# Around both down projections of a two-layer decoder step: one weight split and one gate eviction change their place

## Chip, core, metric

The kernel runs on one core of one Trainium2 chip. The metric is the time of one execution in microseconds (us), lower is better. All engines of the core (PE, which is TensorE; DVE; ACT; POOL; and SP, which here only issues DMAs) run their own instruction lists and meet at semaphores.

## What is computed

Two layers (L = 0 and 1) over 576 tokens (512 of a prompt, 8 x 8 of samples) of width 1024, in float32. Each layer is `x += mixer(rmsnorm(x)); x += convglu(rmsnorm(x))`; the mixer of layer 0 is an mLSTM, that of layer 1 attention with a window. The part of interest is the second half of each layer and what follows the first one:

```
up = h @ w_up                                   # 1024 -> 2 x 2816
g, u = up[..., :D_FF], up[..., D_FF:]
gc = conv_b + sum_j conv_w[j] * gp[:, j:j + T]  # gp: history, then g
y  = (gelu(gc) * u) @ w_down                    # 2816 -> 1024
qkv = rmsnorm(x + y) @ w_qkv                    # after layer 0 only
```

## The kernel before

**Split products.** Each float32 operand is split into a float16 high part (ACT: a scaled copy) and a float16 low part (DVE: operand minus high part), and each product is three matmuls, high x high, high x low, low x high. So every weight tile costs one ACT and one DVE instruction ahead of PE. `split_act` and `split_dve` do it for tiles `stage -> wH, wL` (lines 335 and 341), `block_high` and `block_low` for the blocks of the down projection, `quart` or `mixed -> blk` (lines 406 and 412).

**Up projection.** It runs in 11 steps i = 0 to 10 (KH = 11) of 128 hidden rows of each of two halves s = 0, 1. Steps 1 to 9 use a seven-product scheme in place of eight; steps 0 and 10 are whole: PE makes gate and value of s = 0, then gate and value of s = 1, 48 matmuls each. For each step and s: `gate` (DVE, lines 1052 and 1054) evicts the gate's PSUM to G; `tap` (ACT, L911) starts the convolution; `conv` (DVE, L1064 and L1068) adds the other two taps; `gelu` (ACT, L919 and L920); `hidden` (DVE, L1083) multiplies by the value. Then `turned` (DVE, L1093 to L1099) forms four sums of the step's halves (the tile sums), and the hidden tile is split: `hidden_raw` and `hidden_turned` (ACT, L926, L930) for the high parts, `hidden_lows` (DVE, L1103, L1105) for the low ones. One buffer holds the products of both s (ntmp, h32, h4 are names of it), so the gelu of step i waits until the lows of step i-1 are done.

**Down projection.** It runs over 4 pairs of output tiles, p = 0 to 3, each with 7 block products j = 0 to 6; g = 7p + j counts them, 0 to 27. Block product g is 11 x 3 matmuls (L823) with the weight block g, one of 4 slots. The blocks come from four quarters of the weights (A11, A12, A21, A22) and sums of them: S1 = A21 + A22 (a DMA that accumulates, `pool_s1`), N2 = A11 - A21 (`weight_n2`, DVE, L485), S4 = A12 + N2 (`pool_s4`, a DMA), S3 = N2 + A22 (`weight_s3`, DVE, L491). Block 4 needs S3 and block 5 needs S4. `keep_block` (ACT, L546) copies the PSUM of blocks j = 0, 2, 4 away, before block j + 2 may use the bank; `combine_blocks` (DVE, L519 to L529) adds the rest and adds to x. The last adding is that of g = 27.

**The start of a down projection.** PE does blocks 0 and 1 with the first ten of the eleven k, waits for the lows of step 10, does the eleventh k of both, and goes on with block 2. In layer 1 the eight transposes of the convolution's output rows (L836) stand ahead of block 0, and their two evictions (crow, L1007, ACT) stand on ACT ahead of `keep_block(0)`.

**After layer 0's down projection** PE does the qkv product (L617): 3 chunks of 4 units of 36 matmuls. Before unit 0, ACT splits its tile once block 26 is done, and DVE, after the last adding and after the norm work of x tile 6 (`norm_tile`, L1200 and L1204), makes the low part. Behind unit 0 PE does the column sums of the norm (L1722), which need the norm work of all eight x tiles. All orders are written out by hand: each engine's list is fixed, and nothing overtakes in it.

Of the kernel before, what the change touches and what calls it, by code (L numbers as in the profile page):

```python
# [38 lines left out]
PAIRS = KD // 2  # L39
BLOCKS = 7  # L40
KH = KF // 2
# [45 lines left out]
def build(nc, I, O):  # L87
# [3 lines left out]
    with ctx:  # L91
# [274 lines left out]
        def block_num(L, g):  # L366
            return SEG0[f"down{L}"] + g
# [59 lines left out]
        def up_high(act, L, i, what):  # L427

            j = i + 1
            whole = what in ("g0", "g1") or (isinstance(j, int) and j == KH - 1)  # L430
            first = isinstance(i, int) and i == 0
            if what == "v1" and not whole:
                act.wait_ge(s1_landed, up_s(L, j))
            split_act(act, up_unit(L, j, what), up_base(L, i) + (SLOT[what] + 1 if first else FREED[what]),
                      1 if whole else 2)
# [73 lines left out]
        def block_work(dve, L, g):  # L509

            if g < PAIRS * BLOCKS:
                p, j = divmod(g, BLOCKS)
                block_low(dve, L, g)
                if j == 2:
                    weight_s3(dve, L, p)

        def sum_of(dve, out, a, b, op, done):
# [228 lines left out]
        def pe_ffn(pe, L):  # L746
# [71 lines left out]
            def product(g, ks):  # L818
                p, j = divmod(g, BLOCKS)
                pe.wait_ge(lo_ready, block_num(L, g) + 1)  # L820
                for k in ks:
                    for a, b in THREE:
                        m = nc.tensor.matmul(down_bank(g), blk[:, g % RING, a, 128 * k:128 * (k + 1)],  # L823
                                             (hidH, hidL)[b][:, k, HIDDEN[j], :],
                                             start=(k == 0 and (a, b) == THREE[0] and j in OPENS),
                                             stop=(k == KH - 1 and (a, b) == THREE[2]), skip_group_check=True)
                if ks[-1] == KH - 1:
                    m.then_inc(unit_used, 1)
# [11 lines left out]
            pe.wait_ge(ff["h32"], KF * (L + 1) - 1)  # L840
            pe.wait_ge(mix["low"], KH * L + KH - 1)
            product(0, range(KH - 1))
            product(1, range(KH - 1))
            pe.wait_ge(mix["low"], KH * L + KH)
            product(0, (KH - 1,))
            product(1, (KH - 1,))
            for g in range(2, PAIRS * BLOCKS):
                p, j = divmod(g, BLOCKS)
                if j in (2, 4, 6):
# [55 lines left out]
        def act_ffn(act, L):  # L905
            act.preload_act_table(ACT.Gelu)

            def tap(i, s):
                t, k = KF * L + 2 * i + s, i + KH * s
                act.wait_ge(ff["gate"], t + 3)  # L910
                nc.scalar.activation(acc[:, s, 0:CC], G[:, s, 2:GC], ACT.Identity, bias=pff[:, k, 38 + L:39 + L],  # L911
                                     scale=pff[:, k, 32 + 3 * L + 2:33 + 3 * L + 2]).then_inc(ff["acc"], 1)
# [11 lines left out]
            def hidden_raw(i):  # L924
                act.wait_ge(ff["h32"], KF * L + 2 * i + 2)
                nc.scalar.activation(hidH[:, i, 0:3, :], h4[:, 1:4, :], ACT.Copy).then_inc(mix["raw"], 1)  # L926
# [62 lines left out]
            up_high(act, L, i, "g1")  # L989
            gelu(i, 1)  # L990
            up_high(act, L, i, "v1")
            hidden_raw(i)
            hidden_turned(i)
            block_high(act, L, 0)
            tap(i + 1, 0)
            gelu(i + 1, 0)
            block_high(act, L, 1)
            tap(i + 1, 1)
            gelu(i + 1, 1)
            hidden_raw(i + 1)  # L1000
            hidden_turned(i + 1)
            block_high(act, L, 2)
            block_high(act, L, 3)
            if L:
                act.wait_ge(ctr, 1)
                for lay in range(2):
                    nc.scalar.activation(crow[:, lay, :], PS[0:CONV_ROWS, 4 + lay, :], ACT.Copy).then_inc(cin, 1)  # L1007

            def norm_tile(r):
                m, adds = done_order(r)  # L1010
# [5 lines left out]
            for g in range(PAIRS * BLOCKS):  # L1016
                p, j = divmod(g, BLOCKS)
                keep_block(act, L, g)
                if g + RING < PAIRS * BLOCKS:
                    block_high(act, L, g + RING)  # L1020
                if L == 0:
                    if j == 6:
                        norm_tile(2 * p)
                    if p and j == 0:
                        norm_tile(2 * p - 1)
                    q = g - (PAIRS * BLOCKS - 2)
                    if q == 0:
                        split_act(act, unit("qkv", 0, 0), block_num(0, g) + 1)
                    elif q == 1:
                        for u in range(1, 4):  # L1030
                            split_act(act, unit("qkv", 0, u), block_num(0, g) + 1)
                        norm_tile(2 * p + 1)
                elif p and j in (1, 3):
                    act_stripe(act, 2 * (p - 1) + j // 2)
            if L:
# [4 lines left out]
        def dve_ffn(dve, L):  # L1040
# [57 lines left out]
                dve.wait_ge(mix["t1"], n0 + 2)  # L1098
                nc.vector.tensor_tensor(tmix[:, 3, :], h4[:, 3, :], tmix[:, 2, :], ALU.add).then_inc(mix["sum"], 1)  # L1099

            def hidden_lows(i):
                dve.wait_ge(mix["raw"], KH * L + i + 1)
                nc.vector.tensor_tensor(hidL[:, i, 0:3, :], h4[:, 1:4, :], hidH[:, i, 0:3, :], ALU.subtract)  # L1103
                dve.wait_ge(mix["high"], KH * L + i + 1)
                nc.vector.tensor_tensor(hidL[:, i, 3:7, :], tmix, hidH[:, i, 3:7, :],  # L1105
                                        ALU.subtract).then_inc(mix["low"], 1)

            def value(i, which):

# [64 lines left out]
            up_low(dve, L, i + 1, "g1")  # L1174
            conv(i, 1)
            up_low(dve, L, i + 1, "v1")
            hidden(i, 1)
            turned(i)
            hidden_lows(i)
            block_low(dve, L, 0)  # L1180
            weight_n2(dve, L, 0)
            i = KH - 1
            gate(i, 0)
            conv(i, 0)
            hidden(i, 0)
            gate(i, 1)
            conv(i, 1)
            block_low(dve, L, 1)
            hidden(i, 1)
            turned(i)  # L1190
            hidden_lows(i)
            block_work(dve, L, 2)
            if L == 0:
                dve.wait_ge(mix["low"], KH * L + KH)
                link("V", dve, nc.vector.memset(sqsum[:, :], 0.0))
# [10 lines left out]
            for g in range(PAIRS * BLOCKS):  # L1206
                p, j = divmod(g, BLOCKS)
                if j == 6 and p + 1 < PAIRS:
                    weight_n2(dve, L, p + 1)
                combine_blocks(dve, L, g)  # L1210
                block_work(dve, L, g + 3)
                if L == 0:
                    if j == 6:
                        norm_tile(2 * p)
                    if p and j == 1:
                        norm_tile(2 * p - 1)
                elif p and j in (1, 3):
                    dve_stripe(dve, 2 * (p - 1) + j // 2)
            if L:
                dve_stripe(dve, 2 * PAIRS - 2)  # L1220
                dve_stripe(dve, 2 * PAIRS - 1, 1)
            else:
                split_dve(dve, unit("qkv", 0, 0))
                norm_tile(2 * PAIRS - 1)
                for u in range(1, 4):
                    split_dve(dve, unit("qkv", 0, u))

        def pool_ffn(pool, L):
# [1736 lines left out]
```

## Time and profile before

| | |
|---|---|
| median of 3 runs | 1217.37 us (1217.11 to 1219.19) |
| the profiled execution | 1216.64 us, span 1214.9 us |
| PE busy | 1188.8 us (98%), 9630 matmuls |
| DVE, ACT, POOL busy | 862.9, 613.4, 168.6 us |
| granted TensorE clock, mean | 0.997 |
| chain that ended last | PE 82%, DVE 8%, ACT 4%, issue 2%, DMA 2% |

The span is the time from the first to the last instruction in the trace; 1.74 us lie outside it. PE's granted clock is 1.00 at 2.4 GHz and 0.50 at 1.2 GHz. Times inside a trace count from the span's start. In a timeline row the columns are start, duration, engine, line, operation, out<-in, shape and count; the bracket at the end tells how long the engine stood idle before it and who released it.

### The profile page before, as it was taken

The page shows a single profiled execution, that of the slowest core. Times are in us where ns is not written, and L with a number is a line of the kernel's source. Part 1 is how long each engine was busy: PE and PEld are TensorE (multiplying, and loading weights), DVE is VectorE, ACT ScalarE, POOL GpSimd, SP SyncE. Part 2 cuts the span into 40 slices and gives each one's busy share as a digit, 9 for nine tenths or more (in the row PEclk, how much of TensorE's full clock was granted, in tenths as well). Part 3 has the DMA queues.
Part 4 walks back from the last instruction along what each step waited for, and adds up shares of the span by engine and source line. Part 5 has one row for each costly group of instructions (what it writes and reads, how often), then busy time and mean ns, then how long its engine had stood idle before and what let it go on. Part 6 is the DMA issues. An engine that isn't in the chain of part 4 may idle for free.

```text
span 1214.9 us, 24151 instructions
## 1 busy us (share of the span) xinstructions
PE 1188.8 (98%) x9630; PEld 899.8 (74%) x9630; DVE 862.9 (71%) x1299; ACT 613.4 (50%) x1027; POOL 168.6 (14%) x285
## 2 busy tenths in 40 slices
PE   7999999999999999999998999999999999999998
PEld 6855777777777777777774456687777777777886
DVE  5744567587888888677764479758788878776664
ACT  6322445366555555354444459846555555544432
POOL 1000010002133222000003200000222222200001
PEclk9999999999999999999999999999999999999999
DMA  8643143235645455445546220022755455345563
GB/s 217 239 104 87 53 148 109 75 105 156 158 121 143 116 129 147 120 119 144 148 114 224 82 71 2 2 70 71 199 131 149 110 134 143 86 120 144 148 178 77
DMA packets 197194, 148.60 MB, mean 122 GB/s; under 512 B 5857, under 2 KB 178779, under 8 KB 196530
## 3 DMA queue, kind: packets, MB, share of 16 engines
q1 hardware_dynamic: 181562, 101.80, 29.1%
q0 software_dynamic: 15552, 45.68, 16.0%
q8 instruction: 56, 0.92, 0.3%
q14 instruction: 24, 0.20, 0.0%
HBM read 109.15 MB, written 9.86 MB: 98 GB/s over the span
## 4 chain that ended last, share of the span: by engine, by line
PE 82%; DVE 8%; ACT 4%; issue 2%; DMA 2%; SPq 0%; POOL 0%; DVEq 0%; ACTq 0%; POOLq 0%
PE PS L601 33%; PE PS L823 16%; PE PS L757 15%; PE PS L617 10%; DMA stage<-stage 1%; PE PS L1622 1%; DVE wL L341 1%; PE PS L1642 1%; DVE xT L649 1%; PE PS L1597 1%; DVE P L2649 1%; DVE st L2630 1%; PE PS L1840 1%; ACT wH L335 1%; PE PS L1873 1%
## 5 line engine op out<-in xcount | busy, mean ns | idle before, releaser
L823 PE MATMUL PS<-hidH,blk 128*128 128x288 f16 x1232 | 230.2, 287 | 4.9 <-ACT val L546 2.2
L341 DVE SCALAR_TENSOR_TENSOR wL<-stage,wH 128x1024 f16<-128x1024 f32 x140 | 170.4, 1221 | 82.4 <-ACT wH L335 82.0
L335 ACT ACTIVATE wH<-stage 128x1024 f16<-128x1024 f32 x140 | 146.2, 1049 | 141.7 <-PE PS L617 59.9
L823 PE MATMUL PS<-hidL,blk 128*128 128x288 f16 x616 | 177.1, 288 | 0.0
L601 PE MATMUL PS<-zH,wH 128*128 128x288 f16 x832 | 170.0, 286 | 0.7 <-DVE zL L662 0.7
L601 PE MATMUL PS<-zL,wH 128*128 128x288 f16 x832 | 170.0, 286 | 0.0
L601 PE MATMUL PS<-zH,wL 128*128 128x288 f16 x832 | 170.0, 286 | 0.0
L823 PEld LDWEIGHTS PS<-hidH,blk 128*128 128x128 f16 x1232 | 121.1, 98 | 37.4 <-ACT val L546 3.8
L601 PEld LDWEIGHTS PS<-zH,wH 128*128 128x128 f16 x832 | 81.2, 98 | 22.0 <-DVE zL L662 1.3
L601 PEld LDWEIGHTS PS<-zL,wH 128*128 128x128 f16 x832 | 81.4, 98 | 20.5
L601 PEld LDWEIGHTS PS<-zH,wL 128*128 128x128 f16 x832 | 81.4, 98 | 20.5
L601 PE MATMUL PS<-hnH,wH 128*128 128x288 f16 x396 | 81.0, 287 | 1.8 <-issue 1.2
L406 ACT ACTIVATE blk<-quart 128x1408 f16<-128x1408 f32 x48 | 65.5, 1369 | 32.2 <-DMA quart<-in_w_ffn_down 15.0
L601 PE MATMUL PS<-hnH,wL 128*128 128x288 f16 x396 | 80.9, 286 | 0.0
L601 PE MATMUL PS<-hnL,wH 128*128 128x288 f16 x396 | 80.9, 286 | 0.0
L412 DVE SCALAR_TENSOR_TENSOR blk<-quart,blk 128x1408 f16<-128x1408 f32 x48 | 77.5, 1619 | 0.0
L823 PEld LDWEIGHTS PS<-hidL,blk 128*128 128x128 f16 x616 | 60.5, 98 | 15.2
L519 DVE TENSOR_TENSOR val<-val,PS 128x288 f32<-128x288 f32 x60 | 27.1, 452 | 57.5 <-PE PS L823 32.0
L911 ACT ACTIVATE acc<-G,pff 128x592 f32<-128x592 f32 x44 | 38.7, 879 | 49.6 <-DVE G L1054 49.6
L1242 POOL COPY convO<-G 128x2 f32<-128x2 f32 x44 | 34.1, 774 | 194.3 <-DVE G L1054 194.3
L601 PEld LDWEIGHTS PS<-hnH,wH 128*128 128x128 f16 x396 | 37.8, 98 | 13.3 <-issue 2.1
L617 PE MATMUL PS<-wH,zH 128*128 128x512 f16 (+1 forms) x144 | 44.1, 353 | 3.6 <-DVE wL L341 3.6
(433 smaller groups left out, 2516.6 us busy)
## 6 DMA issues: line engine op xcount, KB each, us to landing
stage<-in_w_ffn_up SPq DMA_DIRECT2D x88, 512.0 KB, 4.2
quart<-in_w_ffn_down SPq DMA_DIRECT2D x32, 704.0 KB, 5.8
stage<-stage POOLq DMA_DIRECT2D x54, 256.0 KB, 4.2
stage<-in_w_mlstm_in SPq DMA_DIRECT2D x24, 512.0 KB, 5.2
stage<-in_w_swa_qkv SPq DMA_DIRECT2D x12, 512.0 KB, 4.6
quart<-quart POOLq DMA_DIRECT2D x8, 704.0 KB, 5.3
quart<-mixed POOLq DMA_DIRECT2D x8, 704.0 KB, 5.3
C<-in_state_mlstm_C POOLq DMA_DIRECT2D x4, 1024.0 KB, 7.4
```

Of the source, the lines that this page charges most:

```text
L335: nc.scalar.activation(wH[:, slot, :], stage[:, slot, :], ACT.Copy, scale=WSCALE).then_inc(hi_ready, inc)
L341: nc.vector.scalar_tensor_tensor(out=wL[:, slot, :], in0=stage[:, slot, :], scalar=WSCALE, in1=wH[:, slot, :], op0=ALU.mult, op1=ALU.subtr ...
L406: nc.scalar.activation(blk[:, g % RING, 0, :], WEIGHT[j], ACT.Copy, scale=WSCALE).then_inc(hi_ready, 1)
L412: nc.vector.scalar_tensor_tensor(out=blk[:, g % RING, 1, :], in0=WEIGHT[g % BLOCKS], scalar=WSCALE, in1=blk[:, g % RING, 0, :], op0=ALU.mu ...
L519: nc.vector.tensor_tensor(out, a, b, op).then_inc(done, 1)
L601: m = nc.tensor.matmul(out[:, hf, :], w[a][:, slot, 128 * (at + j):128 * (at + j + 1)], xs(b, k)[:, HALF * hf:HALF * (hf + 1)], start=(fir ...
L617: m = nc.tensor.matmul(out, x, w[:, cols], start=first, stop=last, skip_group_check=True)
L649: nc.vector.scalar_tensor_tensor(out=halves(xT[:, m, :]), in0=pair(p), scalar=1.0 / WSCALE, in1=halves(xT[:, m, :]), op0=ALU.mult, op1=ALU ...
L757: m = nc.tensor.matmul(up_psum(bank), w[a][:, at + 128 * k:at + 128 * (k + 1)], x(b, k), start=(start and k == 0 and (a, b) == THREE[0]), ...
L823: m = nc.tensor.matmul(down_bank(g), blk[:, g % RING, a, 128 * k:128 * (k + 1)], (hidH, hidL)[b][:, k, HIDDEN[j], :], start=(k == 0 and (a ...
L911: nc.scalar.activation(acc[:, s, 0:CC], G[:, s, 2:GC], ACT.Identity, bias=pff[:, k, 38 + L:39 + L], scale=pff[:, k, 32 + 3 * L + 2:33 + 3 ...
L1242: nc.gpsimd.tensor_copy(convO[:, L, 0:2, k], G[:, s, SEQ:SEQ + 2])
```

## The change

DVE's and ACT's lists at the end of the up projection are put in another order, PE's split between blocks 0 and 1 moves from the tenth to the eighth k of block 1, `weight_s3` of pair 0 goes behind `block_low` of block 3, the crow evictions go behind `keep_block(0)`, and at the end of layer 0 the high part of qkv unit 0 may be made once block 25 is done, its low part stands ahead of the last adding, that of unit 1 behind it. No computation is added or left out.

```diff
@@ block_work
-                if j == 2:
+                if j == (2 if p else 3):
                     weight_s3(dve, L, p)
@@ PE, start of the down projection
             product(0, range(KH - 1))
-            product(1, range(KH - 1))
+            product(1, range(KH - 3))
             pe.wait_ge(mix["low"], KH * L + KH)
             product(0, (KH - 1,))
-            product(1, (KH - 1,))
+            product(1, range(KH - 3, KH))
@@ ACT, end of the up projection (i = 9)
             up_high(act, L, i, "v1")
+            tap(i + 1, 0)
             hidden_raw(i)
             hidden_turned(i)
             block_high(act, L, 0)
-            tap(i + 1, 0)
             gelu(i + 1, 0)
+            tap(i + 1, 1)
             block_high(act, L, 1)
-            tap(i + 1, 1)
             gelu(i + 1, 1)
+            block_high(act, L, 2)
             hidden_raw(i + 1)
             hidden_turned(i + 1)
-            block_high(act, L, 2)
             block_high(act, L, 3)
-            if L:
-                act.wait_ge(ctr, 1)
-                for lay in range(2):
-                    nc.scalar.activation(crow[:, lay, :], PS[0:CONV_ROWS, 4 + lay, :], ACT.Copy).then_inc(cin, 1)
@@ ACT, loop over g
                 keep_block(act, L, g)
+                if L and g == 0:
+                    act.wait_ge(ctr, 1)
+                    for lay in range(2):
+                        nc.scalar.activation(crow[:, lay, :], PS[0:CONV_ROWS, 4 + lay, :], ACT.Copy).then_inc(cin, 1)
...
-                    q = g - (PAIRS * BLOCKS - 2)
-                    if q == 0:
-                        split_act(act, unit("qkv", 0, 0), block_num(0, g) + 1)
-                    elif q == 1:
-                        for u in range(1, 4):
+                    if g == PAIRS * BLOCKS - 2:
+                        split_act(act, unit("qkv", 0, 0), block_num(0, g))
+                    elif g == PAIRS * BLOCKS - 1:
+                        split_act(act, unit("qkv", 0, 1), block_num(0, g) + 1)
+                        norm_tile(2 * p + 1)
+                        for u in range(2, 4):
                             split_act(act, unit("qkv", 0, u), block_num(0, g) + 1)
-                        norm_tile(2 * p + 1)
@@ DVE, end of the up projection (lows_raw, lows_turned: the halves of hidden_lows)
             up_low(dve, L, i + 1, "v1")
+            gate(i + 1, 0)
             hidden(i, 1)
             turned(i)
-            hidden_lows(i)
+            lows_raw(i)
+            conv(i + 1, 0)
+            lows_turned(i)
+            i = KH - 1
             block_low(dve, L, 0)
+            gate(i, 1)
+            hidden(i, 0)
+            conv(i, 1)
             weight_n2(dve, L, 0)
-            i = KH - 1
-            gate(i, 0)
-            conv(i, 0)
-            hidden(i, 0)
-            gate(i, 1)
-            conv(i, 1)
             block_low(dve, L, 1)
             hidden(i, 1)
             turned(i)
             hidden_lows(i)
-            block_work(dve, L, 2)
+            block_low(dve, L, 2)
@@ DVE, loop over g, layer 0
+                    if g == PAIRS * BLOCKS - 2:
+                        split_dve(dve, unit("qkv", 0, 0))
                     if j == 6:
+                        if p == PAIRS - 1:
+                            split_dve(dve, unit("qkv", 0, 1))
                         norm_tile(2 * p)
@@ DVE, after the loop, layer 0
-                split_dve(dve, unit("qkv", 0, 0))
                 norm_tile(2 * PAIRS - 1)
-                for u in range(1, 4):
+                for u in range(2, 4):
                     split_dve(dve, unit("qkv", 0, u))
```

## Rows read from the trace of the kernel before

**Rows 1.** Timeline of PE, start of layer 0's down projection (columns as above)

```profile
520.28 0.29 PE L823 MATMUL PS<-hidH,blk 128*128 128x288 f16 x1
...
524.70 0.30 PE L823 MATMUL PS<-hidH,blk 128*128 128x288 f16 x1 [0.58 <-DVE blk L412]
...
529.73 0.30 PE L823 MATMUL PS<-hidH,blk 128*128 128x288 f16 x1 [1.19 <-DVE hidL L1105]
...
531.36 0.28 PE L823 MATMUL PS<-hidH,blk 128*128 128x288 f16 x1 [0.72 <-DVE blk L412]
```

**Rows 2.** Timeline of PE, end of layer 0's down projection and qkv unit 0

```profile
637.17 0.29 PE L823 MATMUL PS<-hidH,blk 128*128 128x288 f16 x1
641.04 0.39 PE L617 MATMUL PS<-wH,zH 128*128 128x512 f16 x1 [3.58 <-DVE wL L341]
...
645.32 0.38 PE L617 MATMUL PS<-wH,zH 128*128 128x512 f16 x1
...
648.01 0.30 PE L617 MATMUL PS<-wH,zH 128*64 128x256 f16 x2
...
648.78 1.26 PE L1722 MATMUL PS<-C,three 128*128 128x1 f32 x10
```

**Rows 3.** Timeline of PE, start of layer 1's down projection

```profile
1087.91 1.12 PE L836 MATMUL PS<-C,convO 128*99 128x128 f32 x8 [0.57 <-POOL convO L1243]
1088.87 0.29 PE L823 MATMUL PS<-hidH,blk 128*128 128x288 f16 x1
...
1096.67 0.30 PE L823 MATMUL PS<-hidH,blk 128*128 128x288 f16 x1 [0.29 <-DVE hidL L1105]
...
1099.08 0.41 PE L823 MATMUL PS<-hidH,blk 128*128 128x288 f16 x1 [1.50 <-ACT val L546]
```

**Rows 4.** Windows: stretch, length, PE, PEld, DVE, ACT, POOL busy, granted clock, DMA, GB/s

```profile
529.00:530.00 1.00, 0.27 (x3) 0.23 (x4) 1.00 (x2) 1.00 (x2) 0.00 (x0) 1.00 0.88 180
642.00:643.00 1.00, 1.00 (x4) 0.39 (x3) 1.00 (x3) 1.00 (x1) 1.00 (x1) 0.50 1.01 338
693.00:724.00 31.00, 31.00 (x207) 16.98 (x205) 20.21 (x29) 16.53 (x33) 6.83 (x14) 1.00 0.27 77
1100.00:1101.00 1.00, 1.00 (x6) 0.64 (x5) 1.00 (x1) 1.00 (x1) 0.00 (x0) 0.50 0.00 0
```

**Rows 5.** Timeline of DVE, last up step of layer 0

```profile
514.57 0.69 DVE L1052 SCALAR_TENSOR_TENSOR G<-PS,three 128x512 f32<-128x512 f32 x1
...
516.34 0.83 DVE L1064 SCALAR_TENSOR_TENSOR acc<-G,pff,acc 128x592 f32<-128x592 f32 x1 [0.95 <-ACT acc L911]
...
523.02 1.62 DVE L412 SCALAR_TENSOR_TENSOR blk<-quart,blk 128x1408 f16<-128x1408 f32 x1
524.56 0.75 DVE L1083 SCALAR_TENSOR_TENSOR ntmp<-PS,ntmp 128x576 f32<-128x576 f32 x1
...
528.32 1.36 DVE L1105 TENSOR_TENSOR hidL<-three,hidH 128x1152 f16<-128x1152 f32 x1 [0.26 <-ACT hidH L930]
```

**Rows 6.** Timeline of ACT, layers 0 and 1: block 2 kept, crow evicted

```profile
535.60 0.41 ACT L546 ACTIVATE val<-PS 128x288 f32<-128x288 f32 x1 [0.17 <-PE PS L823]
...
1097.66 1.06 ACT L1007 ACTIVATE crow<-PS 99x512 f32<-99x512 f32 x2
...
1105.01 0.41 ACT L546 ACTIVATE val<-PS 128x288 f32<-128x288 f32 x1 [2.64 <-PE PS L823]
```

**Rows 7.** Timeline of DVE and ACT, end of layer 0's down projection and after

```profile
637.50 0.46 DVE L523 SCALAR_TENSOR_TENSOR C<-PS,three 128x288 f32<-128x288 f32 x1 [2.00 <-PE PS L823]
...
639.76 1.22 DVE L341 SCALAR_TENSOR_TENSOR wL<-stage,wH 128x1024 f16<-128x1024 f32 x1
...
655.67 0.17 DVE L2584 TENSOR_SCALAR nsinkb<-sinkb 128x16 f32<-128x16 f32 x1 [9.57 <-DMA sinkr<-in_swa_sinks]
...
637.56 2.95 ACT L335 ACTIVATE wH<-stage 128x1024 f16<-128x1024 f32 x3 [0.68 <-PE PS L823]
```

**Rows 8.** Timeline of PE, block 9 of layer 0

```profile
560.48 0.30 PE L823 MATMUL PS<-hidH,blk 128*128 128x288 f16 x1 [0.66 <-ACT val L546]
```

More of the change, by code:

```diff
@@ L1099, in turned, with lows_raw, lows_turned @@
                 nc.vector.tensor_tensor(tmix[:, 3, :], h4[:, 3, :], tmix[:, 2, :], ALU.add).then_inc(mix["sum"], 1)
-            def hidden_lows(i):
+            def lows_raw(i):
                 dve.wait_ge(mix["raw"], KH * L + i + 1)
                 nc.vector.tensor_tensor(hidL[:, i, 0:3, :], h4[:, 1:4, :], hidH[:, i, 0:3, :], ALU.subtract)
+            def lows_turned(i):
                 dve.wait_ge(mix["high"], KH * L + i + 1)
@@ L1106, in hidden_lows @@
                                         ALU.subtract).then_inc(mix["low"], 1)
+            def hidden_lows(i):
+                lows_raw(i)
+                lows_turned(i)
             def value(i, which):
@@ L1176, in dve_ffn @@
             up_low(dve, L, i + 1, "v1")
+            gate(i + 1, 0)
             hidden(i, 1)
             turned(i)
-            hidden_lows(i)
+            lows_raw(i)
+            conv(i + 1, 0)
+            lows_turned(i)
+            i = KH - 1
             block_low(dve, L, 0)
+            gate(i, 1)
+            hidden(i, 0)
+            conv(i, 1)
             weight_n2(dve, L, 0)
-            i = KH - 1
-            gate(i, 0)
-            conv(i, 0)
-            hidden(i, 0)
-            gate(i, 1)
-            conv(i, 1)
             block_low(dve, L, 1)
```

## The prediction, made before the changed kernel was built or run

> **What bounds the kernel now.** I read the engines' shares first: PE is busy for 98% of the span, so a change can only win what PE loses, in idle time or in clock. Then I read PE's waits and timeline in the three stretches that the change touches, then the granted clock around them, then the other engines' timelines for what released PE.
>
> PE stands three times at the start of layer 0's down projection [rows 1]: for the low part of block 1, for the lows of step 10, for the low part of block 2. It stands once before qkv unit 0, for that unit's low part [rows 2]. In layer 1 it stands for the POOL copies that feed the transposes, for the lows, and for keep_block(0), which is behind the crow evictions on ACT [rows 3]. After two of these places, not after the one in layer 0, the granted clock is 0.50 for a while, which is 1.2 GHz instead of 2.4 [rows 4].
>
> **Pitch.** In rows 3 there are 60 matmuls of blocks 0 and 1 between 1088.87 and 1096.67, with 0.29 idle; in rows 1 there are 30 between 520.28 and 524.70, with 0.58 idle. If a restart costs a fixed d beside the idle time shown, 60p + d = 7.51 and 30p + d = 3.84, so p = 0.122 and d = 0.17 us. The two blocks together, 66 matmuls, take 8.07 us if nothing is waited for.
>
> **Start of layer 0's down projection.** PE begins block 0 at 520.28, without a wait. Nothing that block 0 needs comes later than that in the new order (below). So block 2 can start at 520.28 + 8.07 = 528.35 instead of 531.36: 3.01 us.
>
> Whether it can depends on DVE. The second gate can be evicted when PE is done with it. In the old order the first gate stands at 514.57 [rows 5], directly behind other DVE work. Ahead of that point the change puts that gate and its two conv instructions (0.82 + 1.70) and takes away weight_n2 (1.54 at DVE's pitch) and the 0.85 that it waited for its DMA: 0.13 more, so I leave the second gate at 514.57. Its tap and conv follow as those of the first did, conv 516.34 to 518.04 [rows 5]. Then weight_n2 to 519.5, block_low 1 to 521.1 (1.54 each at pitch; it took 1.62 in rows 5) and hidden(10,1), which needs the value product, done at 520.3, and its gelu, one ACT instruction pair that starts at 518.1. Thus hidden(10,1) starts at 521.05, 3.5 us ahead of 524.56. From its start to the end of the lows was 524.56 to 528.32 + 1.36 = 5.12 [rows 5]; the ACT steps between are the same, except that block_high 2 now stands ahead of hidden_raw; it waits for PE at 520.3 and is over at 521.8, when hidden(10,1) is over too. So the lows are done at 526.2 and block_low 2 at 527.8.
>
> PE wants block 1 at 520.28 + 30p = 523.95 (margin 2.9), the lows after 54 matmuls, at 526.9 (margin 0.7), and block 2 at 528.35 (margin 0.5). Its third condition, keep_block(0), follows the 57th matmul, issued at 527.1: keep_block(2) started 535.60 - 531.36 - 32p = 0.33 after the last matmul of its block [rows 1, 6], so this one lies at 527.5 to 527.9 (margin 0.45). Leaving only the last k to the end would put block 0's end and so this copy 0.7 later, which is what the move from ten to eight k is worth.
>
> Behind that, DVE's list up to block_low 5 is the same set. weight_s3 behind block_low 3 makes block 3 earlier (530.0) and block 4's low part falls at about 534.4, where PE wants it at 528.35 + 8.07 = 536.4. The accumulating DMA of S4 waits for block_low 1 and so goes out 3.5 us earlier. The reload of the first quarter for pair 1 goes out earlier against PE, that of the second some 0.6 us later, those of the last two as before; the last is what pool_s1 and weight_n2 of pair 1 wait for. So I leave the 0.66 wait at block 9 [rows 8] as it is; bounds: it goes (0.8 gained with the restart), or it grows by those 0.6.
>
> **Before qkv unit 0.** PE's last matmul of block 27 is issued at 637.17, so unit 0 could start at 637.29; it starts at 641.04: 3.75 us [rows 2]. ACT made the high part at 633.5, when block 26 was done; the tile had landed by then, so in the new order it is made between 629.9 and 633.5. On DVE the split of unit 0 (1.22, [rows 7]) now stands in the 2.00 us in which DVE waits for block 27 [rows 7], 635.5 to 636.7, margin 0.6. What is queued behind it is the last adding, which waits for PE until 637.5 anyway. PE's other conditions for the first four token tiles are old; the fifth needs one scaling of the last adding, 637.97, and comes 5 us later.
>
> The slow clock goes with the gap: the 12 matmuls from 641.04 to 645.32 took 4.28, the next 12 of the same shape 2.69 [rows 2]: 1.59 us, with the clock at 0.50 [rows 4].
>
> What is late next: the column sums. They would start 637.29 + (648.78 - 641.04) - 1.59 = 643.4. DVE: last adding to 638.45, low part of unit 1 to 639.8 (its high part is the first of the three ACT splits at 637.56, [rows 7]), norm work of tiles 6 and 7, 1.4 each, to 642.7. Margin 0.7. Units 2 and 3 have their low parts by 645.2, PE wants them from 650.5 on. The DMAs issued by POOL behind block 27 keep their time; DVE stands for the last of them until 655.67 [rows 7] and then makes the low part of unit 4, by 657.7; PE reaches that unit at 667.9 - 5.3 = 662.6. Later in qkv PE is busy all the time in its last 31 us [rows 4] and ACT and DVE follow it, so the gain is carried.
>
> **Start of layer 1's down projection.** The value product's end is 1087.91 - 0.57 - 0.17 = 1087.17. The last gate is out 5 us earlier, so the POOL copies are too. Transposes 1088.87 - 1087.91 = 0.96, then 8.07: block 2 at 1096.20 instead of 1099.08: 2.88 us [rows 3]. DVE's chain is that of layer 0 without the 0.54 memset and ends, against PE, 0.96 earlier. The 1.06 of crow [rows 6] now stand between keep_block(0) and block_high 4, which waits 1.7 us longer for weight_s3 anyway; PE wants block 4 at 1104.3 and it is there at about 1100.8.
>
> Here too the clock was at 0.50 [rows 4]. From the start of block 2 to its copy it took 4.24 in layer 0 and 5.93 in layer 1 [rows 1, 3, 6]: 1.69 us.
>
> A page of the Trainium skill speaks against counting this last term: "TensorE: Matmul & The Clock Gate", Part 1, says that the monitor's window runs free of the kernel, so that where a slow stretch falls varies from run to run. The rows leave it open: gaps of 0.58, 1.19 and 0.72 in layer 0 brought no fall of the clock, and 0.57, 0.29 and 1.50 in layer 1 did.
>
> **Sum.** 3.01 + 3.75 + 1.59 + 2.88 + 1.69 = 12.92 us. Against the profiled execution's 1216.64 that is 1203.7; this execution lies 0.73 below the median of 1217.37, against which it is 1204.4. I take 1204.2.
>
> **Rivals.**
> - *Margins too thin.* Four margins of 0.45 to 0.7 us at layer 0's start, one at 0.6 and one at 0.7 around unit 0. For it: each rests on a chain of six to ten hand-overs. Against: the durations are those of the same instructions between the same engines. If they fail, PE waits 0.3 to 1.5 at two or three places and the clock may fall once (1.6): 1205.5 to 1208. Chance 0.17.
> - *The clock doesn't come back.* A slow stretch stays or appears behind a smaller gap, such as that at block 9. One costs 1.6, two 3.3: 1205.8 to 1207.5. For it: layer 1's fall came after small gaps. Against: the gaps themselves are gone. Chance 0.08.
> - *The qkv gain is given back* in attention, to a transfer or a POOL task that keeps its time after block 27. It would cost up to 5.3: 1209.5. Against: DVE's and ACT's waits there end on PE. Chance 0.04.
> - *The change doesn't do what it says*, because another condition had ended together with the one removed (the value's hidden tile, the weight's landing): 1210 to 1217. Chance 0.02.
> - *Slower.* weight_n2 stands ahead of block_low 1, hidden(10,1) and the lows, and it waits for the accumulating DMA of S1. That landed at 513.0 and is now wanted at 518.0. Nothing is lost until 518.9; from there each us costs one in each layer, and both layers' falls of the clock are there. The gain outside is 3.75 + 1.59, so with x us lost at each start the sign turns where 2(x - 2.95) + 1.6 = 5.34, the 1.6 being a fall in layer 0 too: x = 4.8, a landing at 523.7. At 526 it is 1217.4 + 4.6 = 1222. Against: 11 us of delay, with nothing else on the DMA queues at that time. Chance 0.02.
>
> **Numbers.** The forecast has 0.67, its own range 1202.8 to 1205.5. The range for 8 in 10 takes in block 9's wait gone below, thin margins and one or two clock falls above: 1202.6 to 1208.2. Within 0.2% (about what a measurement of this kernel can tell) means above 1214.9: 0.02; slower by more 0.02; faster 0.96.
>
> **What would show it.** PE's timeline without a wait from 520 to the first matmul of block 9 in layer 0, unit 0 directly behind block 27, layer 1's block 2 at 9.0 after the value product's end; clock 1.00 in all three stretches; hidden(10,1) 0.8 after the value product's end. Wrong would be: a PE wait for L1105, L412 or L546 before block 3; a wait of the column sums; a wait in attention that was not there.

## The result, and the profile after

The changed kernel takes 1203.81 us (median of 4 runs, 1203.35 to 1204.61), the kernel before in the same series 1217.33 (1217.11 to 1219.19): a ratio of 0.9886, 95% interval [0.9869, 0.9903]. The forecast was 1204.2. The profiled execution took 1204.14 with a span of 1202.3; it is 12.50 under that of before, where the sum had 12.92.

PE's timeline in layer 0: first and 67th matmul of the down projection (the second of the pair at 529.19, so 529.31, is the first of block 2), block 9, the last of block 27, then the first and the thirteenth of qkv unit 0 and the column sums. Columns as in the rows of before.

```profile
521.23 0.29 PE L823 MATMUL PS<-hidH,blk 128*128 128x288 f16 x1
...
529.19 0.41 PE L823 MATMUL PS<-hidH,blk 128*128 128x288 f16 x2
...
558.02 0.30 PE L823 MATMUL PS<-hidH,blk 128*128 128x288 f16 x1 [0.25 <-ACT val L546]
...
634.72 0.29 PE L823 MATMUL PS<-hidH,blk 128*128 128x288 f16 x1
634.84 0.38 PE L617 MATMUL PS<-wH,zH 128*128 128x512 f16 x1
...
637.43 0.38 PE L617 MATMUL PS<-wH,zH 128*128 128x512 f16 x1
...
640.89 1.26 PE L1732 MATMUL PS<-C,three 128*128 128x1 f32 x10
```

The three brackets of [rows 1] are gone, and so is the 3.58 of [rows 2]: unit 0 is issued 0.12 behind block 27. The first twelve matmuls of unit 0 take 2.59 us where they took 4.28. In layer 1 the transposes, the first block and the first matmuls of block 2 (1088.24) follow each other the same way, against the three brackets of [rows 3]:

```profile
1079.29 1.04 PE L836 MATMUL PS<-C,convO 128*99 128x128 f32 x8
1080.16 0.29 PE L823 MATMUL PS<-hidH,blk 128*128 128x288 f16 x1
...
1088.12 0.41 PE L823 MATMUL PS<-hidH,blk 128*128 128x288 f16 x2
```

Windows of the changed kernel in the three stretches (columns as in [rows 4]): the third number from the end is the granted clock, and it is 1.00 in each.

```profile
529.00:530.00 1.00, 1.00 (x10) 0.80 (x9) 0.96 (x2) 0.00 (x0) 0.00 (x0) 1.00 0.00 0
636.00:637.00 1.00, 1.00 (x7) 0.41 (x6) 0.81 (x1) 1.00 (x3) 1.00 (x2) 1.00 1.04 379
1091.00:1092.00 1.00, 1.00 (x10) 0.80 (x9) 0.68 (x1) 1.00 (x2) 0.00 (x0) 1.00 1.12 340
```

All of PE's waits that are left between 500 and 1215 us (releaser, us in total, times, longest):

```profile
PE PS L1850 <- DVE P L2659: 1.4, 3, 0.7
PE PS L1809 <- ACT st L2170: 1.3, 2, 0.9
PE PS L601 <- issue: 1.2, 1, 1.2
PE PS L1821 <- ACT qS L1349: 0.6, 1, 0.6
PE PS L887 <- DVE xT L529: 0.3, 1, 0.3
PE PS L823 <- ACT val L546: 0.2, 1, 0.2
PE PS L601 <- DVE zL L662: 0.2, 1, 0.2
```

Only the one of 0.2 for `val` (block 9) lies in the stretches that were touched. The others stand in attention and after it and stood there before, with the same lengths within 0.1.

**Where the 12.6 us of span went.** Each line is the distance between two marks of PE (the sixth row ends at keep_block(2) on ACT) in either trace; together they cover the execution.

| from - to | before | after | gain | forecast |
|---|---|---|---|---|
| start - first matmul of block 0, layer 0 | 520.28 | 521.23 | -0.95 | 0 |
| - block 2 | 11.08 | 8.08 | 3.00 | 3.01 |
| - block 9 | 29.12 | 28.71 | 0.41 | 0 |
| - qkv unit 0 | 80.56 | 76.82 | 3.74 | 3.75 |
| - column sums | 7.74 | 6.05 | 1.69 | 1.59 |
| - transposes - block 2, layer 1 - keep_block(2) | 439.13, 11.17, 5.93 | 438.40, 8.95, 4.25 | 0.73, 2.22, 1.68 | 2.88, 1.69 |
| - end | 109.89 | 109.81 | 0.08 | 0 |

In layer 1 the 0.73 and 2.22, together 2.95, stand for the forecast's 2.88. The 0.95 lost ahead of block 0 is not the change's: it arises before 300 us, where both kernels are the same (0.7 of it is a wait of PE for a transfer of tL at 299). In eight traces of kernels with the new order at the end of the up projection block 0 begins between 520.06 and 522.28, in six with the old order between 520.28 and 521.34.

**The margins.** DVE's timeline at layer 0's start, with the second gate first, then hidden(10,1), the lows and block_low 2 (last columns: idle time and releaser):

```profile
515.63 0.69 DVE L1052 SCALAR_TENSOR_TENSOR G<-PS,three 128x512 f32<-128x512 f32 x1 [0.51 <-PE PS L601]
...
522.09 0.75 DVE L1083 SCALAR_TENSOR_TENSOR ntmp<-PS,ntmp 128x576 f32<-128x576 f32 x1
...
525.85 1.36 DVE L1107 TENSOR_TENSOR hidL<-three,hidH 128x1152 f16<-128x1152 f32 x1 [0.26 <-ACT hidH L930]
527.13 1.62 DVE L412 SCALAR_TENSOR_TENSOR blk<-mixed,blk 128x1408 f16<-128x1408 f32 x1
```

And around unit 0: its low part, the last adding, unit 1's low part, and the end of the norm work of tile 7.

```profile
632.96 1.22 DVE L341 SCALAR_TENSOR_TENSOR wL<-stage,wH 128x1024 f16<-128x1024 f32 x1
635.04 0.46 DVE L523 SCALAR_TENSOR_TENSOR C<-PS,three 128x288 f32<-128x288 f32 x1 [0.87 <-PE PS L823]
...
636.19 1.23 DVE L341 SCALAR_TENSOR_TENSOR wL<-stage,wH 128x1024 f16<-128x1024 f32 x1 [0.20 <-ACT wH L335]
...
639.46 0.75 DVE L1211 TENSOR_TENSOR three<-three,ntmp 128x576 f32<-128x576 f32 x1
```

The lows are done at 527.21 and PE wants them 54 matmuls after 521.23, at 527.83: margin 0.62 (forecast 0.7). block_low 2 is done at 528.75 for 529.31: 0.56 (0.5). Unit 0's low part is done at 634.18 for 634.84: 0.66 (0.6). The norm work ends at 640.21 for 640.89: 0.68 (0.7). The smallest margin is that of keep_block(0), on ACT's timeline; it is over at 528.88, for 529.31: 0.43 (0.45).

```profile
528.47 0.41 ACT L546 ACTIVATE val<-PS 128x288 f32<-128x288 f32 x1 [1.39 <-PE PS L823]
```

### The profile page after: what moved, and what is told of

It is laid out like the page before. It is cut to its first block, busy times and chain, and to the rows that moved or that the text cites. A ratio compares the mean times of both kernels' runs of the same rounds, so it can differ in the third digit from the quotient of the medians.

```text
span 1202.3 us, 24151 instructions
## 1 busy us (share of the span) xinstructions
PE 1183.9 (98%) x9630; PEld 899.1 (75%) x9630; DVE 861.8 (72%) x1299; ACT 613.9 (51%) x1027; POOL 175.6 (15%) x285
## 4 chain that ended last, share of the span: by engine, by line
PE 86%; DVE 6%; ACT 4%; issue 2%; DMA 2%; POOL 0%; SPq 0%; DVEq 0%; POOLq 0%; ACTq 0%
PE PS L601 34%; PE PS L823 17%; PE PS L757 15%; PE PS L617 10%; DMA tL<-hidH 1%; PE PS L1632 1%; PE PS L1652 1%; DVE xT L649 1%; PE PS L1607 1%; DVE P L2659 1%; ACT ntmp L657 1%; DVE st L2640 1%; PE PS L1850 1%; PE PS L1883 1%; ACT wH L335 1%
## 5 line engine op out<-in xcount | busy, mean ns | idle before, releaser
L1252 POOL COPY convO<-G 128x2 f32<-128x2 f32 x44 | 39.0, 887 | 193.1 <-DVE G L1054 193.1
L601 PEld LDWEIGHTS PS<-hnH,wL 128*128 128x128 f16 x396 | 38.7, 98 | 9.8
```

The costliest lines, as they stand in the source:

```text
L601: m = nc.tensor.matmul(out[:, hf, :], w[a][:, slot, 128 * (at + j):128 * (at + j + 1)], xs(b, k)[:, HALF * hf:HALF * (hf + 1)], start=(fir ...
L1252: nc.gpsimd.tensor_copy(convO[:, L, 0:2, k], G[:, s, SEQ:SEQ + 2])
```

## Experiments

**1. The qkv order undone, and the qkv order alone.** The same lines, taken out of the changed kernel and put into the kernel before.

```diff
@@ DVE, loop over g, layer 0 (and the splits of ACT and DVE after it, likewise)
-                    if g == PAIRS * BLOCKS - 2:
-                        split_dve(dve, unit("qkv", 0, 0))
...
+                split_dve(dve, unit("qkv", 0, 0))
                 norm_tile(2 * PAIRS - 1)
```

> The changed kernel with only the order at the end of layer 0 as before (qkv unit 0 split after the last adding). Theory of the prediction: PE waits 3.6 us again before unit 0 and runs the first 12 matmuls at the low clock, so 3.75 + 1.6 = 5.35 us come back: 1203.8 + 5.35 = 1209.2, with clock 0.50 for some 3 us behind the gap and none of the stalls at the two starts. Rival (the slow clock belongs to this place, to the DMA load or the wide matmuls, not to the gap): the changed kernel's trace would have shown it; here only 3.75 come back, 1207.6. Rival (the parts are not independent): outside 1208.5 to 1210.

> The kernel before with only the order at the end of layer 0 changed. Theory: 3.75 + 1.6 = 5.35 us less, 1217.3 - 5.35 = 1212.0; unit 0 directly behind block 27 at full clock, the stalls at both starts of the down projections unchanged, layer 1's with the clock at 0.50 behind it. Rival (the fall of the clock in layer 1 depends on where in time the gap falls and not on the gap): with everything there shifted by 5.35 us it may be gone, 1210.3.

Undone: 1209.75 (6 runs, 1206.46 to 1210.82), ratio to the kernel before 0.9935 [0.9916, 0.9953]. Alone: 1210.8 (6 runs, 1210.25 to 1211.58), ratio 0.9948 [0.9931, 0.9965]; the kernel before had 1215.58 (23 runs) in this series. PE's timeline of the first has the old gap back and nothing else; its thirteenth matmul of unit 0 comes 4.29 later, and neither layer's start has a wait:

```profile
639.84 0.39 PE L617 MATMUL PS<-wH,zH 128*128 128x512 f16 x1 [3.58 <-DVE wL L341]
```

The second has unit 0 directly behind block 27, twelve matmuls in 2.59, and the old waits of 0.45, 1.18 and 0.72 in layer 0 and 0.70, 0.29 and 1.50 in layer 1. Layer 1's slow stretch is there too, 5 us earlier in time than before: keep_block(2) follows block 2 by 5.92 (1094.02 to 1099.94), which speaks against the rival that the fall hangs on the moment. So the part at qkv is worth some 5.9 us by the first kernel (1209.75 against 1203.81, which is of another series) and 4.8 by the medians of the second (6.3 by its ratio), forecast 5.34; the starts have the rest. Medians of one kernel differ between series by over 1 us (the kernel before: 1215.58 to 1217.33), so these runs do not show more closely that the parts add up.

**2. The crow evictions alone.** Into the kernel before: crow behind keep_block(0).

```diff
@@ ACT
-            if L:
-                act.wait_ge(ctr, 1)
-                ... crow
             for g in range(PAIRS * BLOCKS):
                 keep_block(act, L, g)
+                if L and g == 0:
+                    ... crow
```

> The kernel before with only the two crow evictions of layer 1 moved behind keep_block(0). keep_block(0) then ends at 1098.1 instead of 1099.0, where the low part of block 2 ends too (1098.15), so block 2 starts 0.9 us earlier and PE's last idle time shrinks from 1.50 to about 0.6. Theory A (the fall of the clock hangs on the length of the last gap): it goes, 1.7 more, together 2.6: 1214.7. Theory B (it hangs on all three gaps together, or on something else): it stays, 1216.4.

1215.04 (12 runs, 1212.28 to 1217.51), ratio 0.9985 [0.9972, 0.9998]. PE's timeline shows the last gap of layer 1 go from 1.50 to 0.72, now behind block_low 2:

```profile
1101.18 0.28 PE L823 MATMUL PS<-hidH,blk 128*128 128x288 f16 x1 [0.72 <-DVE blk L412]
```

keep_block(2) follows 4.24 later (1105.42), so the clock stayed up there. But in the same trace it fell in layer 0, where the gaps were 0.39, 1.19 and 0.71 as always; the window's granted clock:

```profile
532.00:535.00 3.00, 3.00 (x15) 1.92 (x14) 2.90 (x3) 1.99 (x2) 0.00 (x0) 0.52 0.02 5
```

So a fall does not belong to one certain gap, and the median (0.54 under the kernel before, by the ratio 1.8) cannot tell the two forecasts apart.

**3. The qkv gap filled.** Into the kernel before: 26 matmuls whose product nobody reads, so that PE works in the gap and unit 0 still starts when its low part comes.

```diff
@@ PE, behind layer 0's down projection
             pe_ffn(pe, 0)
+            pe.wait_ge(added, PAIR_ADDS * (PAIRS - 1) + 1)
+            for _ in range(26):
+                nc.tensor.matmul(PS[:, 7, 0:HALF], zH[:, 0, 0:128], zH[:, 0, 0:HALF], start=True, stop=True)
```

> The kernel before with 26 matmuls of 288 columns, whose results nobody reads, between block 27 and qkv unit 0 (26 x 0.122 = 3.2 us in the 3.75 us gap). Nothing else changes, so unit 0 starts when it did. Theory (the low clock behind the gap is the price of the idle PE): unit 0 runs at full clock and 1.6 to 1.7 us are gained: 1215.7. Rival (it has another cause, such as the DMA burst that starts there): 1217.3.

1213.65 (12 runs, 1212.86 to 1217.09), ratio 0.998 [0.9968, 0.9992], that is 1.93 under the kernel before by the medians (forecast 1.6). Unit 0 started 0.40 after the last useless matmul and ran at full clock (twelve in 2.60). So the clock's part at qkv is real and separate from the idle time: 1.7 in the trace (2.60 in place of 4.28) with the distance from block 27 to unit 0 unmoved, 3.87 us. The median is no measure of that part alone. Here too something was not as forecast. Layer 1 had its gap of 1.50 (1097.81), yet keep_block(2) came at 1102.07, 4.26 later, and the window shows no fall:

```profile
1098.00:1102.00 4.00, 4.00 (x35) 3.19 (x34) 4.00 (x5) 2.64 (x2) 0.00 (x0) 1.00 0.15 41
```

And 7 of the 12 executions had a mean granted clock of 1.000, in which no fall of the usual length fits (experiment 6). So layer 1's fall was absent from them too, and the 1.93 may hold some of it.

**4. The three small moves undone** in the changed kernel: PE's split point, weight_s3, crow.

```diff
-                if j == (2 if p else 3):
+                if j == 2:
...
-            product(1, range(KH - 3))
+            product(1, range(KH - 1))
...
-                if L and g == 0:
-                    ... crow        (back ahead of the loop over g)
```

> The changed kernel with its three small moves undone: PE's split after ten k of block 1 instead of eight, weight_s3 of pair 0 ahead of block_low 3, crow evictions ahead of keep_block(0). Theory: block 0 ends 8 matmuls later (63 instead of 57, less two of the tail: 0.7 us) and keep_block(0) with it, so block 2 starts 0.3 us later in each layer, the trace shows a wait of 0.1 to 0.3 for L546 there, and the time is 1204.4, not to be told from 1203.8. Rival (the small moves carry a share of their own, crow above all): over 1205.5.

1204.46 (6 runs, 1203.33 to 1208.34); the changed kernel in this series, below, had 1204.25. PE's timeline:

```profile
530.18 0.30 PE L823 MATMUL PS<-hidH,blk 128*128 128x288 f16 x1 [0.19 <-ACT val L546]
...
1089.98 0.30 PE L823 MATMUL PS<-hidH,blk 128*128 128x288 f16 x1 [0.20 <-ACT val L546]
```

As worked out: keep_block(0) comes 0.7 later than in the changed kernel against a margin of 0.43, and PE waits for it, 0.19 and 0.20. Layer 0 has no crow and waits as long as layer 1, so this wait is that of the split point. ACT's timeline in layer 1 shows that crow has no part in it: it is evicted by 1087.49, and keep_block(0) then stands 2.02 for PE.

```profile
1086.43 1.06 ACT L1007 ACTIVATE crow<-PS 99x512 f32<-99x512 f32 x2
1089.52 0.41 ACT L546 ACTIVATE val<-PS 128x288 f32<-128x288 f32 x1 [2.02 <-PE PS L823]
```

So the move of crow, worth 0.8 of idle time in the old order (experiment 2), is worth nothing in the new one. One of the six executions took 1208.34 at a mean clock of 0.998, so a slow stretch seems to come at times in this order too; there is no trace of it.

**5. How firm the margins are.** One, then three useless DVE instructions of 1.62 us ahead of hidden(10,1), in both layers.

```diff
             weight_n2(dve, L, 0)
             block_low(dve, L, 1)
+            ... waits that keep the buffer safe
+            for _ in range(1):      # or 3
+                ... scalar_tensor_tensor, 128x1408, into the low part of block 2
             hidden(i, 1)
```

> The changed kernel with one useless DVE instruction of 1.62 us (1.67 with its hand-over) between block_low 1 and hidden(10,1) in both layers; it delays the lows of step 10 and the low part of block 2. Measured margins of the changed kernel: lows 0.62 and low part 0.56 in layer 0, 1.57 and 1.5 in layer 1. So block 2 starts 1.15 later in layer 0 and 0.3 later in layer 1: 1205.3, without a fall of the clock. Rival (margins are larger, since something else hides it): 1203.8. Rival (even a gap of 1 us costs the clock): 1207.

> As the one before with three such instructions, 5.0 us. Block 2 starts 4.45 later in layer 0 and 3.5 later in layer 1, 8.0 together, with PE idle 4.3 and 3.4 us ahead of the last k of blocks 0 and 1. Theory (a gap of that length costs the clock, 1.7 each time): 1215.2. Rival (it doesn't): 1211.8. If the chain behind block 2 has slack that takes part of it: under 1211.

One: 1205.91 (4 runs, 1205.24 to 1205.97), ratio 0.9915 [0.9901, 0.993]; that is 1.7 over the changed kernel in this series, of which the gap in the trace explains 0.9. Three: 1214.39 (10 runs, 1213.24 to 1216.6), ratio 0.9988 [0.9978, 0.9998]; of the 10.1 over the changed kernel the two gaps in the trace are 7.6 and its one fall about 1.5. The execution with the trace was the fastest of the ten; eight of the others have a lower mean clock (0.995 to 0.997 against 0.998), so they lost more to slow stretches. PE's timeline of the first, then of the second:

```profile
528.12 0.30 PE L823 MATMUL PS<-hidH,blk 128*128 128x288 f16 x1 [0.92 <-DVE hidL L1107]
```

```profile
531.07 0.42 PE L823 MATMUL PS<-hidH,blk 128*128 128x288 f16 x1 [4.24 <-DVE hidL L1107]
...
1095.73 0.30 PE L823 MATMUL PS<-hidH,blk 128*128 128x288 f16 x1 [3.36 <-DVE hidL L1107]
```

3 x 1.62 less the margin of 0.62 is 4.24; one instruction gives 0.92 in layer 0 and nothing in layer 1. There the forecast had the chain 0.96 earlier, a margin of 1.58: 4.86 - 1.58 = 3.28, measured 3.36. So the margin of the lows, read from the timeline, is a true one in both layers: DVE's chain through hidden(10,1) is what PE would wait for next, and from there each us costs one. The clock after the two gaps of the second kernel:

```profile
532.00:535.00 3.00, 3.00 (x18) 2.04 (x16) 2.90 (x4) 0.41 (x1) 0.00 (x0) 0.65 0.00 0
1096.00:1100.00 4.00, 4.00 (x34) 3.03 (x32) 4.00 (x3) 1.38 (x3) 0.00 (x0) 1.00 0.01 3
```

It fell behind the 4.24 and stayed at 1.00 behind the 3.36. Neither expectation had that mixture, and by the mean clocks it is that of one execution, not of the kernel.

**6. The kernels once more.** The changed kernel in two more series, and two more profiled executions of the kernel before.

> The changed kernel once more, as the yardstick of this batch: 1203.8, and no PE wait over 0.3 us at the two starts nor before qkv unit 0. Where the kernel before spread over 7 us in the batch before (1213.4 to 1220.2), theory of the slow clock: its three gaps bring a fall in some executions and not in others, so a kernel without the gaps spreads over no more than 2 us. Rival: the spread comes from the transfers before layer 0's up projection, then this kernel spreads alike.

> The changed kernel again, as the yardstick of keep_first: 1204.2, between 1203.3 and 1205.8. Theory (falls of the clock belong to gaps): no granted clock of 0.50 in any of the three stretches. Rival (a fall can come anywhere): one of them shows 0.50 and the execution is 1.7 us longer.

> The kernel before, one more profiled execution, to see which of its gaps bring a fall of the clock. Theory (a fall costs 1.7 us and comes behind the short gaps in some executions only): the gap of 3.6 us ahead of qkv brings one again; behind the short gaps of layers 0 and 1 the clock falls or not, and the execution's time is near 1213.3 + 1.7 for each fall there. Rival (each gap has its fixed outcome): exactly as in the first profile, a fall in layer 1 and none in layer 0, 1216.6.

> The same once more: the qkv gap brings a fall; of the short gaps in layers 0 and 1 none, one or both, with about 1213.3, 1215.0 or 1216.7 us. By the rival 1216.6 with the fall in layer 1 alone.

The changed kernel: 1204.25 (4 runs, 1203.82 to 1205.82), ratio 0.99 [0.9886, 0.9915], and 1203.26 (5 runs, 1203.04 to 1204.65), ratio 0.9892 [0.9875, 0.9909]. Neither trace has a slow stretch. The kernel before: 1217.53 and 1217.15. Both have the fall at qkv and in layer 1 (block 2 to its copy 5.92 each time) and none in layer 0, as the first trace: where the falls are, the three traces agree with the rival of the fixed outcome. How long they are does not. Windows of 635 to 655, the first profiled execution of the kernel before and then the last:

```profile
635.00:655.00 20.00, 16.42 (x91) 8.44 (x88) 8.84 (x11) 8.77 (x15) 10.43 (x19) 0.91 0.76 249
```

```profile
635.00:655.00 20.00, 16.42 (x84) 8.13 (x83) 8.42 (x11) 8.77 (x15) 10.46 (x19) 0.83 0.77 252
```

A mean clock that is 0.09 or 0.17 short over 20 us is 1.8 or 3.4 us short, but a part of the second slow stretch lies in the gap itself, where nothing is lost. PE's timeline gives what was lost, first matmul of unit 0 to column sums in the last trace:

```profile
640.63 0.61 PE L617 MATMUL PS<-wH,zH 128*128 128x512 f16 x1 [3.58 <-DVE wL L341]
641.03 0.63 PE L617 MATMUL PS<-wH,zL 128*128 128x512 f16 x1
...
649.33 1.26 PE L1722 MATMUL PS<-C,three 128*128 128x1 f32 x10
```

That is 8.70, where the first trace has 7.74 and the changed kernel 6.05: 2.65 and 1.69 lost behind the same gap of 3.58. Here the first matmul is slow already (the second is issued 0.40 behind it); in the first trace the clock fell only behind the third.

Slow clock in the traces, by gap: behind 3.58 at qkv in 5 of 5 (2.6 us lost in two of them, 1.7 in three); behind 4.24 in 1 of 1; behind 3.36 in 0 of 1; behind layer 1's three gaps ending in 1.50 in 4 of 5; behind layer 0's three (about 0.5, 1.19, 0.72) in 1 of 6; behind layer 1's ending in 0.72 in 0 of 1; behind 0.92 in 0 of 1.

Each run also has a mean granted clock, so all executions can be sorted by it, the profiled ones included:

| kernel, mean clock | executions | median us | range |
|---|---|---|---|
| before, 0.999 to 1.000 | 12 | 1214.15 | 1213.35 to 1216.74 |
| before, 0.997 to 0.998 | 25 | 1216.13 | 1214.47 to 1217.88 |
| before, 0.994 to 0.996 | 17 | 1218.47 | 1216.33 to 1220.22 |
| before, all | 54 | 1216.46 | 1213.35 to 1220.22 |
| changed, 0.999 to 1.000 (all) | 13 | 1203.83 | 1203.04 to 1205.82 |

One execution of the kernel with the qkv order undone had a mean clock of 1.000 and took 1206.46, the other five 1209.07 to 1210.82: so even the gap of 3.58 seems to pass without a fall at times. Four of the 54 executions of the kernel before have 1.000 as well (median 1214.29). A fall that loses 1.7 us is some 3.4 us at half speed and takes 0.0014 off the mean, so none fits into a mean that rounds to 1.000, but one fits into 0.999: the profiled execution of the qkv order alone has 0.999 and the fall in layer 1. For none of the executions without a fall at qkv is there a trace.

**7. Block 9's wait.** In the changed kernel, for pairs 1 to 3 of layer 0, ACT's norm work of tile 2p - 2 goes behind keep_block of the pair's first block.

```diff
@@ ACT, loop over g
+                if L == 0 and p and j == 0:
+                    norm_tile(2 * p - 2)
                 if g + RING < PAIRS * BLOCKS:
                     block_high(act, L, g + RING)
                 if L == 0:
-                    if j == 6:
+                    if j == 6 and p == PAIRS - 1:
                         norm_tile(2 * p)
```

> In the changed kernel PE still stands 0.25 to 0.8 us at block 9 of layer 0, because keep_block(7) on ACT is queued behind the norm work of x tile 0. Here, for pairs 1 to 3 of layer 0, ACT's norm work of tile 2p-2 stands behind keep_block of the pair's first block instead of ahead of it. Theory (ACT's order alone makes this wait): PE's timeline shows no wait at block 9, and the time is 0.3 to 0.8 us under the changed kernel of the same batch, about 1203.5. Rival (DVE's low part or the weight landing ends just as late): the wait stays under another name, and the time is that of the changed kernel within 0.2 us.

1203.18 (5 runs, 1202.75 to 1204.38), ratio 0.9894 [0.9876, 0.9911], against 1203.26 of the changed kernel in the same series. In the trace PE has no wait at all between 500 us and attention, from the first matmul of block 0 (520.28) to unit 0 at 633.47: 113.19, where the three traces of the changed kernel, with 0.25, 0.76 and 1.06 at block 9, have 113.61, 114.13 and 114.53. So the mechanism is shown and is worth 0.4 to 1.3 in one execution. That the median is better is not shown: 0.08 us lies far inside either spread, and what is won here is as large as what varies ahead of block 0.

## Why the prediction was right

**Starts of the down projections: right in mechanism and size.** 3.00 for 3.01 in layer 0, 2.95 for 2.88 in layer 1. The sum rested on PE running 66 matmuls without a gap at the pitch of 0.122, and on a DVE chain put together from rows of the old order. The prediction says four margins of 0.45 to 0.7 here, but works out three (lows, block_low 2, keep_block(0)); these came out within 0.1 of the forecast, as did the two around unit 0. Experiment 5 shows for the lows that the margin is what it was taken for, and experiment 4 for keep_block(0); the two around unit 0 were not tested. The second gate came 5.60 ahead of block 0 where the forecast had 5.71, behind 0.51 of waiting for PE.

**The gap before qkv: right.** 3.74 for 3.75. Experiment 1 shows it alone and undone. The high part was made at once when block 25 was done (627.32, that is 7.52 ahead of unit 0; the early end of the forecast, 629.9, lay 7.39 ahead); the tile had landed by then.

**The slow clock behind it: right for the trace compared, 0.1 too small.** 1.69 for 1.59: the twelve fast matmuls that were used for comparison reached into a change of tile (2.69), the same twelve at full clock take 2.59. Experiment 3 shows this term by itself. In two of the five traces with this gap it was 2.6, so the single trace was a guess at its size.

**Layer 1's slow clock: right for the pair of traces compared, and a chance term.** 1.68 for 1.69. But the fall comes behind the same gaps in some executions and not in others. The rule cited from the Trainium skill, "TensorE: Matmul & The Clock Gate", Part 1, agrees with the traces: whether a slow stretch follows the same gaps varies between executions, and so does its length (experiments 2, 3 and 6). By the table of experiment 6 the gain over all executions, 1216.46 - 1203.83 = 12.6, is 10.3 at a clock of 0.999 to 1.000 and 2.3 from the clock, where the sum had 9.64 and 3.28. (With the executions at 1.000 alone it is 10.2: 1214.29 less 1204.14.) So the clock's two terms, taken from one trace that had both falls, were by this estimate about 1 us too large for a median, and block 9 with what else had been put at nothing made up for part of it. That the total came out within 0.4 is in part luck. So is the 13.5 between the two medians of the result's own series: 1217.33 is the highest of the four medians of the kernel before.

**Block 9: the cost put at nothing was 0.4 in this execution,** inside the bounds named. Its size changes from trace to trace of either kernel (0.66, 0.40 and 0.22 before, 0.25, 0.76 and 1.06 after), so no gain there is shown. Experiment 7 names its cause: keep_block(7) is queued on ACT behind the norm work of tile 0.

**Nothing was given back.** From the column sums to layer 1's transposes PE's distance is 439.13 before and 438.40 after, and the difference is the wait for POOL that layer 1's start lost. Of the rivals, "margins too thin" needs 0.6 us more of DVE work to come true, and "slower" the 4 to 5 us of experiment 5: the kernel with three useless instructions is back at 0.9988.

## What to carry to other kernels

Where the bounding engine waits at a hand-over between stages, read from its timeline when it could have started, and put together the other engines' chain in the new order from the durations of the old one; the margins that came out here were good to 0.1 us, and they say what is late next. Before a slow clock is counted as a term, look at it in several executions: here one fall costs 1.7 us or 2.6, and comes or stays away behind the same gap, so it belongs in the sum with its frequency, and the kernel without the gaps also spreads less (1213.4 to 1220.2 before, 1203.0 to 1205.8 after). What a move is worth depends on the order around it: the move of crow took 0.8 us of idle time away in the old order and nothing in the new one.

## What the runs showed that was not expected

POOL's two copies of the tail of the last step's first gate now fall beside DVE's tile sums, directly behind POOL's issue of S1's accumulating DMA. POOL's timeline, then DVE's:

```profile
508.66 0.86 POOL L501 DMA_DIRECT2D quart<-quart  x1 [4.79 <-DMA quart<-in_w_ffn_down]
509.20 0.56 POOL L1252 COPY convO<-G 128x2 f32<-128x2 f32 x1
509.32 1.44 POOL L1253 COPY convO<-G 128x16 f32<-128x16 f32 x1
```

```profile
509.64 1.05 DVE L1103 TENSOR_TENSOR hidL<-ntmp,hidH 128x864 f16<-128x864 f32 x1
```

The copies of the gate before take 0.19 and 0.22 (498.86 and 498.99). The second of the two shown ends at 510.76, just behind DVE's instruction with two inputs from SBUF (510.69). "SBUF - State Buffer" of the Trainium skill, in its section on the two separate sides, has DVE's operations with two SBUF inputs and GpSimd's reads take turns on one pair of ports; that fits. The DMA issue ahead of the copies could be the cause as well, but the traces speak against it. In both layers of all eight traces with the new order the first copy ends 0.02 to 0.03 behind the end of such a DVE instruction and the second 0.05 to 0.07 behind the end of the next one, while the second copy's end lies 2.06 to 2.73 behind the start of the DMA issue. The longest is layer 1 of the last trace of the changed kernel, where the issue comes later against DVE and each copy ends with an instruction one further on. POOL's timeline, then DVE's:

```profile
1067.35 0.85 POOL L501 DMA_DIRECT2D quart<-quart  x1 [4.90 <-DMA quart<-in_w_ffn_down]
1067.89 1.41 POOL L1252 COPY convO<-G 128x2 f32<-128x2 f32 x1
1068.29 1.79 POOL L1253 COPY convO<-G 128x16 f32<-128x16 f32 x1
```

```profile
1068.22 1.05 DVE L1103 TENSOR_TENSOR hidL<-ntmp,hidH 128x864 f16<-128x864 f32 x1
1069.19 0.83 DVE L1064 SCALAR_TENSOR_TENSOR acc<-G,pff,acc 128x592 f32<-128x592 f32 x1
```

No run moves the copies or the DMA issue, so the cause is read from times and not tested. It cost nothing: in layer 1 the second copy, of the same length, starts at 1067.38, and the transposes follow at 1079.29.
